# On-chip tiles that begin at multiples of 64 bytes instead of 32, in a two-layer encoder trunk

## The chip, the cores and the metric

The kernel runs on one core of one Trainium2 chip. The metric is the time of one execution on the device in microseconds (us), as the median of several runs. A profile is one execution taken by the hardware profiler; its span is the time from the first to the last instruction.

## The reference, cut to what matters

The computation is a float32 trunk of two layers over x of shape (1, 512, 1024). Each layer has a mixer with a residual add and then a feed-forward with a residual add:

```
for layer in range(2):
    h = rmsnorm(x, mix_norm[layer])
    if layer == 0:   # z = h @ e_w_in; gated short convolution (512 wide) beside
                     # sliding-window attention (8 q heads, 2 kv heads, ALiBi, sinks)
        y = concat(rmsnorm(ya, g[:512]), rmsnorm(yb, g[512:])) @ e_w_out
    else:            # z = h @ o_w_in; spatial gating over 128 positions beside
                     # latent attention (cq 384 wide, ckv 256 wide, 8 heads, rotary key)
        y = concat(rmsnorm(yc, g[:512]), rmsnorm(yd, g[512:])) @ o_w_out
    x = x + y
    h = rmsnorm(x, ffn_norm[layer])
    gate, up = split(h @ w_ffn_in[layer], 2)        # 1024 -> 2 x 2816
    x = x + (silu(gate) * up) @ w_ffn_out[layer]    # 2816 -> 1024
return x
```

## The kernel before, in words

Activations lie transposed: features on the 128 partitions, the 512 positions along the partition, so a tile of one feature block is [128, 512] float32, 2048 bytes per partition. xT holds the residual stream in 8 such blocks.

Every large product is made from three matmuls. Each operand is split in a high part, rounded to the type float32r, and a low part, the rest, in float32r too. `product` issues high x high, high x low and low x high into the same PSUM bank (lines 1506, 1507 and 1508). One operand is stationary in TensorE, the other one, 512 columns as a rule, is streamed through it (the moving operand). For plain float32 products (means of squares at line 1537, attention scores at 1881 and 1595, attention values at 1907 and 1617, the gating mix at 1870) one matmul is made in two passes. Transposes (1544, 1582, 1605, 1782, 1896, 1958) hold the data stationary and stream the identity, which is part of the tile small.

Weights come in 188 loads. SyncE's queue brings one into one of the two slots of raw, ScalarE copies it to w_hi (line 650), VectorE writes w_lo = raw - w_hi (line 1038), and TensorE uses the load (function `load`). There are four slots of w_hi and w_lo. Semaphores order this: a slot is refilled when TensorE has used it, and a raw slot when VectorE has read it. Each of the five engines runs one list of instructions in the order written, and the order around the loads is written out by hand (`through` converts up to four loads ahead).

The stages in order: x is loaded into x_tok and transposed; the first layer's projections stream h_hi and h_lo over the weights; attention and convolution of layer 0; output group over yb and ya (`out_group`); first half of the feed-forward (h streamed, 22 blocks of hidden features in act_hi and act_lo); second half (act streamed), in two passes over the output features. Layer 1 repeats this with cq and ckv as latent tiles, yc and yd ahead of the output group. In one place (columns of the spatial gate's v, loads O_CV) h is stationary and the weights stream.

The tiles' places are given by hand. `sb` places tiles one behind another from `base`: xT, h_hi, h_lo, raw, w_hi, w_lo, small, tables, gains, mix0_gain, gate_bias, sinks, eps_col, spare, mask_q, mask_k, tiny, row_scale, acc, sq, y0, rs. Behind them begins the region R (`R = place[0]`, line 160), in which the stages' tiles are laid over one another at R plus multiples of 1024 bytes: act_hi, act_lo, x_tok, e_sc, yb_hi, yb_lo, alibi, e_q, conv_y, ya_hi, cq, ckv, yc, yd, o_q, o_k, o_pT, v_c and so on. ffn_t lies over sq and y0. out_tok lies over h_hi. In the profile y0 is printed as y and mix0_gain as mix_gain.

The sizes that matter, in bytes per partition: xT 16384, h_hi and h_lo 16384 each, raw 8192, w_hi and w_lo 16384 each, small 3072, tables 6144, gains 268, mix0_gain 32, gate_bias 2048, sinks 32, eps_col 4, spare 4, mask_q and mask_k 256 each, tiny 512, row_scale and acc 2048 each, sq, y0 and rs 4096 each. The first byte that the allocator leaves free is 16481, and the end is 229344; with act_hi and act_lo (2 x 45056 bytes) behind R, the tiles reach 225824 before the change.

Of the kernel before, what the change touches and what calls it, by code (L numbers as in the profile page):

```python
# [106 lines left out]
def program(nc, x, mix_norm, ffn_norm, w_ffn_in, w_ffn_out, e_w_in, e_conv, e_q_gain, e_k_gain,  # L107
# [1 line left out]
            o_q_a_gain, o_kv_a_gain, o_w_uq, o_w_ukv, o_q_gain, o_k_gain, o_out_gain, o_w_out,  # L109
            c_small, c_tables, c_alibi, out):  # L110
    ctx = ExitStack()
    base = (nc.sbuf_base + 31) // 32 * 32
    top = nc.sbuf_top
    place = [base]

    def at(name, shape, dt, offset):
        return nc.alloc_sbuf_tensor_at(name, shape, dt, offset=offset)

    def sb(name, shape, dt=F32, size=4):
        n = size  # L120
        for d in shape[1:]:
            n *= d
        t = at(name, shape, dt, place[0])
        place[0] += (n + 31) // 32 * 32
        return t


    xT = sb("xT", [P, DT, S])
    h_at = place[0]
    h_hi = sb("h_hi", [P, DT, S], F32R)  # L130
    h_lo = sb("h_lo", [P, DT, S], F32R)
    out_tok = at("out_tok", [P, QT, D], F32, h_at)

# [1890 lines left out]
```

## Time and profile before

| what | value |
|---|---|
| median of 3 runs | 1178.49 us (1176.54 to 1180.4) |
| span of the profiled execution | 1177.5 us |
| mean granted TensorE clock | 0.995 |
| TensorE busy (matmul) | 1146.0 us, 97% |
| TensorE weight loads, beside it | 904.4 us |
| VectorE, ScalarE, GpSimd busy | 579.2, 440.9, 117.8 us |
| HBM read | 101.23 MB, 88 GB/s over the span |

How to read the rows: PE is TensorE (matmul), PEld its weight loads, DVE VectorE, ACT ScalarE, POOL GpSimd. A group of instructions names the line of the kernel, the operation, what it writes and behind the arrow what it reads; for a matmul the moving operand stands first and the stationary one second. "389" in such a row is the mean duration of one in ns. Matmuls overlap, so that the distance between two starts is shorter than the duration of one. In the chain of work that ended last each piece has its start and what it adds to the chain.

### The profile page before, as it was taken

What the parts mean: (1) busy time and instruction counts of PE and PEld (TensorE: products, weight loads), DVE (VectorE), ACT (ScalarE), POOL (GpSimd) and SP (SyncE); (2) the same over time, 40 slices, a digit from 0 to 9 for tenths busy, and PEclk for the clock granted to TensorE, in tenths of its full rate; (3) what the DMA queues carried; (4) which work ended last, traced back from release to release, by engine and by line L of the source; (5) the groups of instructions that cost most, each with busy time, mean ns of one, the idle gap of its engine ahead of it and who ended that gap; (6) DMA issues with size and microseconds to landing.
All of it is one profiled execution on the core that took longest, in us unless ns stands there. A gap on an engine that the chain in (4) does not pass through costs nothing.

```text
span 1177.5 us, 13729 instructions
## 1 busy us (share of the span) xinstructions
PE 1146.0 (97%) x5059; PEld 904.4 (77%) x5059; DVE 579.2 (49%) x796; ACT 440.9 (37%) x681; POOL 117.8 (10%) x154
## 2 busy tenths in 40 slices
PE   7999899999999999999999989999999999999998
PEld 6777668888888888888877744578888888888886
DVE  6578876534434333242675786565343443432321
ACT  5545444423223222131546666543332332321220
POOL 5010200001001000000204120000110100100000
PEclk9999999999999999999999999999999999999999
DMA  6522132232332323332323210023323323223230
GB/s 184 188 60 68 55 87 90 90 107 89 98 98 89 107 89 93 102 91 72 91 73 92 73 50 3 1 84 96 107 90 95 101 89 107 89 95 101 81 117 36
DMA packets 84983, 103.87 MB, mean 88 GB/s; under 512 B 10579, under 2 KB 61456, under 8 KB 84816
## 3 DMA queue, kind: packets, MB, share of 16 engines
q1 hardware_dynamic: 81792, 101.99, 28.5%
q10 hardware_dynamic: 2096, 1.05, 0.3%
q8 instruction: 25, 0.41, 0.2%
q0 software_dynamic: 1056, 0.30, 0.1%
q14 instruction: 14, 0.11, 0.0%
HBM read 101.23 MB, written 2.10 MB: 88 GB/s over the span
## 4 chain that ended last, share of the span: by engine, by line
PE 89%; DVE 7%; ACT 2%; DMA 1%; issue 1%; POOL 0%; SPq 0%; DVEq 0%; ACTq 0%; POOLq 0%
PE ps L1506 27%; PE ps L1507 27%; PE ps L1508 27%; PE ps L1881 2%; PE ps L1537 2%; PE ps L1907 2%; DMA x_tok<-in_x 1%; DVE e_sc L1187 1%; PE ps L1896 1%; ACT e_sc L738 1%; DVE e_sc L1176 1%; DVE tiny L1168 1%; PE ps L1883 0%; DVE e_pT L1195 0%; DVE conv_y L1236 0%
## 5 line engine op out<-in xcount | busy, mean ns | idle before, releaser
L1038 DVE TENSOR_TENSOR w_lo<-raw,w_hi 128x1024 fp32r<-128x1024 f32 (+2 forms) x194 | 228.0, 1180 | 453.9 <-ACT w_hi L650 450.9
L650 ACT ACTIVATE w_hi<-raw 128x1024 fp32r<-128x1024 f32 (+2 forms) x194 | 196.1, 1017 | 493.3 <-PE ps L1508 476.6
L1506 PE MATMUL ps<-h_hi,w_hi 128*128 128x512 f32 x928 | 367.1, 396 | 0.7 <-DVE conv_h L1207 0.6
L1508 PE MATMUL ps<-h_hi,w_lo 128*128 128x512 f32 x928 | 361.4, 389 | 0.0
L1507 PE MATMUL ps<-h_lo,w_hi 128*128 128x512 f32 x928 | 361.3, 389 | 0.0
L1506 PEld LDWEIGHTS ps<-h_hi,w_hi 128*128 128x128 f32 x928 | 174.4, 188 | 42.0 <-issue 4.6
L1507 PEld LDWEIGHTS ps<-h_lo,w_hi 128*128 128x128 f32 x928 | 174.3, 188 | 38.2 <-issue 2.6
L1508 PEld LDWEIGHTS ps<-h_hi,w_lo 128*128 128x128 f32 x928 | 174.2, 188 | 36.3
L1506 PE MATMUL ps<-act_hi,w_hi 128*128 (+1 forms) x352 | 139.6, 397 | 0.0
L1508 PE MATMUL ps<-act_hi,w_lo 128*128 (+1 forms) x352 | 139.6, 396 | 0.0
L1507 PE MATMUL ps<-act_lo,w_hi 128*128 (+1 forms) x352 | 139.5, 396 | 0.0
L543 POOL TENSOR_TENSOR ffn_t<-ffn_t,row_scale 128x512 f32<-128x512 f32 x40 | 50.8, 1291 | 558.2 <-ACT ffn_t L815 558.2
L1508 PEld LDWEIGHTS ps<-act_hi,w_lo 128*128 128x128 f32 x352 | 66.3, 188 | 16.2
L1507 PEld LDWEIGHTS ps<-act_lo,w_hi 128*128 128x128 f32 x352 | 66.3, 188 | 16.1
L1506 PEld LDWEIGHTS ps<-act_hi,w_hi 128*128 128x128 f32 x352 | 66.3, 188 | 16.1
L1290 DVE TENSOR_TENSOR ffn_t<-ps,ffn_t 128x512 f32<-128x512 f32 x44 | 30.4, 692 | 44.7 <-POOL ffn_t L543 40.6
L818 ACT ACTIVATE act_hi<-ffn_t 128x512 f32 (+1 forms) x44 | 27.8, 633 | 49.2 <-DVE ffn_t L1290 49.2
L815 ACT ACTIVATE ffn_t<-ffn_t 128x512 f32<-128x512 f32 x44 | 27.0, 633 | 39.0 <-DVE ffn_t L1286 39.0
L1293 DVE TENSOR_TENSOR act_lo<-ffn_t,act_hi 128x512 f32 (+1 forms) x44 | 30.2, 687 | 6.5 <-ACT act_hi L818 6.3
L1881 PE MATMUL ps<-o_k,o_q 128*128 128x512 f32 (+3 forms) x64 | 27.2, 509 | 4.5 <-ACT o_p L970 3.1
L1262 DVE TENSOR_TENSOR xT<-ps,xT 128x512 f32<-128x512 f32 x32 | 20.8, 682 | 20.2 <-PE ps L1508 20.2
L1286 DVE TENSOR_TENSOR ffn_t<-ps,row_scale 128x512 f32<-128x512 f32 x44 | 28.2, 681 | 0.0
(247 smaller groups left out, 1083.2 us busy)
## 6 DMA issues: line engine op xcount, KB each, us to landing
raw<-in_w_ffn_in SPq DMA_DIRECT2D x88, 512.0 KB, 3.5
raw<-in_w_ffn_out SPq DMA_DIRECT2D x44, 512.0 KB, 3.8
raw<-in_e_w_in SPq DMA_DIRECT2D x18, 512.0 KB, 3.7
raw<-in_o_w_in SPq DMA_DIRECT2D x8, 512.0 KB, 3.7
raw<-in_o_w_out SPq DMA_DIRECT2D x8, 512.0 KB, 3.6
raw<-in_e_w_out SPq DMA_DIRECT2D x8, 256.0 KB, 3.9
raw<-in_e_w_out SPq DMA_DIRECT2D x4, 512.0 KB, 4.0
out_dram<-out_tok SPq DMA_DIRECT2D x8, 256.0 KB, 3.6
```

The costliest lines, as they stand in the source:

```text
L543: pool.tensor_tensor(ffn_t[:, t, :], ffn_t[:, t, :], row_scale[:, :], ALU.mult).then_inc(silu_scaled, 1)
L650: ins = act.activation(dst, src, ACT.Copy)
L815: act.activation(ffn_t[:, b, :], ffn_t[:, b, :], ACT.Silu).then_inc(silu_done, 1)
L818: act.activation(dst[:, t, :], ffn_t[:, (t0 + t) % 4, :], ACT.Copy).then_inc(hidden_hi, 1)
L1038: ins = TT(dst, src, high, ALU.subtract)
L1286: TT(ffn_t[:, (t0 + t) % 4, :], ps[:, b0 + t, :], row_scale[:, :], ALU.mult).then_inc(gate_scaled, 1)
L1290: TT(ffn_t[:, b, :], ps[:, b0 + 2 + t, :], ffn_t[:, b, :], ALU.mult).then_inc(hidden_ready, 1)
L1293: TT(dst_lo[:, t, :], ffn_t[:, (t0 + t) % 4, :], dst_hi[:, t, :].bitcast(F32), ALU.subtract).then_inc(hidden_lo, 1)
L1506: MM(dst, st_hi, mv_hi, start=start, stop=False)
L1507: MM(dst, st_hi, mv_lo, start=False, stop=False)
L1508: return MM(dst, st_lo, mv_hi, start=False, stop=stop)
L1881: MM(s_, o_q[:, h, i * P:(i + 1) * P], o_k[:, h, 0:P * (i + 1)], start=True, stop=False)
```

## The change

Two roundings are changed: that of the first tile's start, and that of each tile's size when the next one is placed by `sb`. Tiles placed in region R are given as R plus a number and move with R. Nothing else is changed.

```diff
-    base = (nc.sbuf_base + 31) // 32 * 32
+    base = (nc.sbuf_base + 63) // 64 * 64
     top = nc.sbuf_top
     place = [base]
...
         t = at(name, shape, dt, place[0])
-        place[0] += (n + 31) // 32 * 32
+        place[0] += (n + 63) // 64 * 64
         return t
```

## Rows read from the trace of the kernel before

**Rows 1.** The page, part 1: busy time and share of each engine.
```profile
PE 1146.0 (97%) x5059; PEld 904.4 (77%) x5059; DVE 579.2 (49%) x796; ACT 440.9 (37%) x681; POOL 117.8 (10%) x154
```

**Rows 2.** The page, part 4: the chain that ended last, by engine.
```profile
PE 89%; DVE 7%; ACT 2%; DMA 1%; issue 1%; POOL 0%; SPq 0%; DVEq 0%; ACTq 0%; POOLq 0%
```

**Rows 3.** Groups, shapes apart, TensorE: line, names, shape, count | busy, mean ns | idle.
```profile
L1507 PE MATMUL ps<-h_lo,w_hi 128*128 128x512 f32 x928 | 361.3, 389 | 0.0
...
L1507 PE MATMUL ps<-act_lo,w_hi 128*128 128x512 f32 x96 | 38.0, 396 | 0.0
...
L1507 PE MATMUL ps<-yc_lo,w_hi 128*128 128x512 f32 x32 | 12.7, 396 | 0.0
...
L1507 PE MATMUL ps<-w_lo,h_hi 128*128 128x512 f32 x32 | 12.5, 390 | 0.0
...
L1507 PE MATMUL ps<-cq_lo,w_hi 128*128 128x512 f32 x24 | 9.5, 396 | 0.0
...
L1507 PE MATMUL ps<-w_lo,ckv_hi 128*128 128x256 f32 x16 | 4.5, 281 | 0.0
...
L1507 PE MATMUL ps<-ckv_lo,w_hi 128*128 128x512 f32 x8 | 3.2, 395 | 0.0
```

**Rows 4.** Timeline, TensorE, 300 to 340 us: first and last of 178 (start, us).
```profile
299.79 0.39 PE L1506 MATMUL ps<-h_hi,w_hi 128*128 128x512 f32 x1
...
339.91 0.39 PE L1506 MATMUL ps<-h_hi,w_hi 128*128 128x512 f32 x1
```

**Rows 5.** Timeline, TensorE, 500 to 540 us: first and last of 173.
```profile
499.65 0.39 PE L1506 MATMUL ps<-act_hi,w_hi 128*128 128x512 f32 x1
...
539.95 0.39 PE L1507 MATMUL ps<-act_lo,w_hi 128*128 x1
```

**Rows 6.** Chain in order of time (start, us, what): float32 means, and transposes.
```profile
634.44 1.72 PE ps L1537 x4
...
610.58 0.87 PE ps L1782 x8
```

**Rows 7.** Groups, shapes apart, ScalarE (y is y0).
```profile
L650 ACT ACTIVATE w_hi<-raw 128x1024 fp32r<-128x1024 f32 x170 | 179.5, 1057 | 471.9 <-PE ps L1508 455.2 <-DMA raw<-in_e_w_in 9.9 <-DMA raw<-in_o_w_in 4.1
...
L676 ACT ACTIVATE sq<-xT 128x512 f32<-128x512 f32 x32 | 19.7, 618 | 1.2 <-DVE acc L1069 1.1
...
L692 ACT ACTIVATE rs<-y 128x512 f32<-128x512 f32 x28 | 17.7, 632 | 3.2 <-POOL o_q L590 0.9
...
L650 ACT ACTIVATE w_hi<-raw 128x512 fp32r<-128x512 f32 x12 | 6.7, 621 | 0.0
...
L751 ACT ACTIVATE sq<-yb 128x512 f32<-128x512 f32 x4 | 2.5, 632 | 0.1
```

**Rows 8.** Groups, shapes apart, VectorE.
```profile
L1038 DVE TENSOR_TENSOR w_lo<-raw,w_hi 128x512 fp32r<-128x512 f32 x12 | 7.6, 685 | 0.0
...
L1047 DVE TENSOR_TENSOR yb_lo<-yb,yb_hi 128x512 fp32r<-128x512 f32 x4 | 2.7, 692 | 0.1
...
L1249 DVE TENSOR_TENSOR conv_y<-ps,conv_y 128x512 f32<-128x512 f32 x4 | 2.5, 680 | 0.0
```

**Rows 9.** Timeline, TensorE: idle time and its releaser, around the output groups.
```profile
157.50 1.10 PE L1537 MATMUL ps<-acc,small 128*128 128x512 f32 x2 [2.03 <-DVE acc L1080]
...
164.40 0.50 PE L1506 MATMUL ps<-ya_hi,w_hi 128*128 128x512 f32 x1 [0.19 <-DVE ya_lo L1047]
...
769.69 0.50 PE L1506 MATMUL ps<-yd_hi,w_hi 128*128 128x512 f32 x1 [0.41 <-DVE yd_lo L1047]
```

**Rows 10.** Chain, 672 to 714 us: where it leaves TensorE.
```profile
674.63 2.16 PE ps L1870 x37
676.79 0.66 DVE k_pair_a L1403
```

**Rows 11.** Windows: us, busy (x) of PE, PEld, DVE, ACT, POOL, PEclk, DMA, GB/s.
```profile
688.00:702.00 14.00, 10.58 (x39) 5.24 (x40) 12.30 (x25) 12.30 (x26) 1.39 (x2) 1.00 0.12 39
702.00:712.00 10.00, 10.00 (x21) 3.70 (x20) 8.04 (x16) 5.36 (x18) 2.12 (x1) 0.50 0.17 53
```

**Rows 12.** Chain, the start of the kernel.
```profile
2.23 9.97 DMA x_tok<-in_x
```

## The prediction

> **What bounds the kernel now.** I read four views. The page's first part says who is busy: TensorE holds 97% of the span, the next engine 49% [rows 1]. The chain of work that ended last confirms that this is the bound and not only activity: 89% of it is TensorE, 7% VectorE, 2% ScalarE [rows 2]. So anything that shortens a matmul on that chain is worth its full price, and anything on another engine is worth only what lies in the 9%. Then the groups of instructions with shapes kept apart, because a layout change can only show as a different duration of the same instruction on another tile [rows 3, 7, 8]. Last the timeline, for the distance from one start to the next, since the printed durations overlap (about 0.39 us long, 0.23 us apart) and only the distance is paid [rows 4, 5].
>
> **Where the tiles lie.** The allocator's first free byte is 16481; rounded up to 32 or to 64 it is 16512, so the first tile does not move. xT, h_hi, h_lo, raw, w_hi, w_lo, small and tables have sizes in multiples of 64, so none of them moves: they begin at 0 past a 64-byte line before and after. gains (268 bytes) is the first whose rounding changes. From gains at 115840 the sizes before are 288 + 32 + 2048 + 32 + 32 + 32 + 256 + 256 + 512 = 3488, so row_scale begins at 119328, which is 32 past a line. Everything after it has sizes in multiples of 1024, and every tile placed by hand from R is a multiple of 1024 behind R = 135712: acc, sq, y0, rs, ffn_t and the whole region R are 32 past a line. After the change the same sum is 320 + 64 + 2048 + 64 + 64 + 64 + 256 + 256 + 512 = 3648, a shift of 160 bytes: row_scale is at 119488 and R at 135872, both 0 past a 64-byte line (and, for a rival below, 64 past a 128-byte line). No instruction, wait or transfer is added or removed. The whole effect is what one start address costs an instruction.
>
> **The main term: moving operands of the three-product matmuls.** In the groups the first name behind the arrow is the operand that streams (moving), the second the stationary one. With a stream from h or w (both at 0) the mean is 389 and 390 ns; with a stream from act, yc, cq or ckv (all at 32) it is 396, 396, 396 and 395 [rows 3]. All have 512 columns and the same pair of types. The streams at 32 stand in four different stages (both output groups, the latent projections, the feed-forward's second half), those at 0 in the two others, so the stage is not what they share. The distances say the same: in the first half of the feed-forward 177 steps from 299.79 to 339.91 us, 226.7 ns each [rows 4]; in the second half 172 steps from 499.65 to 539.95 us, 234.3 ns each [rows 5]. That is 7.6 ns by distances and 7 by means; I take 7.3.
>
> Is 7.3 ns what a shift by half a 64-byte line should cost? A stream of 256 columns takes 281 ns and one of 512 takes 390, so a column costs 109/256 = 0.43 ns, and 7.3 ns are 17 columns, or 68 bytes [rows 3]. A run of 2048 bytes that begins half-way in a 64-byte line touches 33 lines instead of 32: one line more, 16 columns. ScalarE gives a second witness that knows nothing of TensorE: Square of 512 elements takes 618 ns from xT (at 0), but 632 from y0 and 632 from yb (both at 32); its cost per element is (1057 - 621)/512 = 0.85 ns, so 14 ns are again 16 elements [rows 7]. It also separates address from place, as y0 lies in the fixed part and yb in region R, and both cost the same.
>
> Count of such products: act 1056 (44 loads of 24), yb, ya, yc and yd 96 each, cq 72, ckv 24, together 1536. Not all are on the chain. In the first output group 48 products with yb end in waits: TensorE waits 2.03 us for acc and then 0.19 us for ya_lo [rows 9]. In the last load of yc before yd_lo (24 products) it waits 0.41 us [rows 9]. 12 of ckv run ahead of a stretch which the chain gives to VectorE [rows 10]. Those 84 gain nothing: the wait behind them grows by what they save. What is left is 1452 x 7.3 ns = 10.6 us. Nothing new comes late in the second half of the feed-forward: a load there would take 24 x 227 ns, which is what one takes in the first half, where the same converting work and more runs on VectorE and ScalarE and TensorE has no gap [rows 4].
>
> **The other terms.** The plain float32 products (means, scores, values) stream at another rate. Four passes of 512 columns from tiles at 32 take 1.72 us, 430 ns each; eight passes of 128 columns that stream the identity, at 0, take 0.87 us, 109 ns each [rows 6]. Between them a column costs (430 - 109)/384 = 0.836 ns, and what is left over is 2 ns for either, so a start at 32 costs these nothing I can see; bound 0 to 2 ns on the 340 or so passes of all their groups, 0 to 0.7 us, taken as 0. A stationary operand at 32 (ckv, 48 products) has no twin at 0 with 256 columns; at most the same 7 ns, 0.3 us, taken as 0. ScalarE: 2% of the chain is 24 us, of which at most 14/632 goes, 0.5 us; those of its steps that read PSUM gain nothing, so 0.4 [rows 2, 7]. VectorE: one read from PSUM and one from a tile at 32 takes 680 ns, two reads from tiles at 32 692, two at 0 685 [rows 8]; 0 to 7 ns of about 690 on 82 us of chain is 0 to 0.8 us, taken as 0. GpSimd's products are hidden, since the instructions behind them wait under TensorE's stream. The load of x into region R stands alone at the start, 9.97 us [rows 12]; no row compares starts for a DMA, so I bound it by TensorE's own 1.8% either way, 0.2 us, taken as 0. The clock: between 702 and 712 us the granted clock is 0.50, behind a stretch in which TensorE was busy for 10.58 of 14 us [rows 11]; the change shortens this stretch by 0.1 us at most, so I leave the drop where it is.
>
> Sum: 10.6 + 0.4 = 11.0 us. Against the profiled execution, 1177.5 us of span, that is 1166.5. The median of the runs is 1178.49, which is 1.0 above this span, so the forecast is 1167.5 us.
>
> **A rule that speaks against it.** The rows show a cost for a start at 32. The Trainium skill ("SBUF — State Buffer", in the notes under Door 1) states lines of 16 bytes for SBUF, with a price for each access that crosses to a new line; by it 32 and 64 are both whole lines, the sum would be 0, and the time 1178.5. The rows differ, as 396 against 389 ns shows. The same page ("Operand start alignment") only says what starts are legal and that its runs timed nothing.
>
> **The rivals.**
> 1. The start is not the cause. If the 7 ns came from something else that region R's tiles share (their place high in the partition, or the neighbour that writes them), or only a multiple of 128 bytes is a good start, nothing is gained: all tiles that now stream fast begin at 0 past a 128-byte line too, and after the change region R begins at 64 past one. Time 1178.5. For it: no row has a stream that begins at 64 past 128, so the trace can't exclude it. Against it: y0 and yb agree although only one is in R [rows 7], and an extra line of 128 bytes would be 32 columns, 13.8 ns, twice what is measured. This is also what would be seen if the change did not move the tiles as I computed.
> 2. Slower: the cost grows with the bytes ahead of the start within a 128-byte line. Then 32 bytes cost 7.3 ns and 64 cost 14.6; all 1452 products on the chain pay 7.3 more, 10.6 us, and the time is 1189.1. It decides if the memory fetches 128 bytes at a time and throws the head away. Against it: 32 bytes are 8 columns, which at 0.43 ns are 3.4 ns, half of the measured.
> 3. The clock. The drop of 10 us at half speed costs 5 us of work [rows 11]. If the slightly shorter wait keeps the clock up, the time is 1162.5; if the shift makes another such stretch, in the attention of the first layer, 1172.5.
>
> **How the numbers follow.** The forecast, 1167.5, has a chance of 0.82; rival 1 0.09; rival 2 0.03; rival 3 0.03 on either side. The range takes in the bounds (7.0 to 7.6 ns, the 0.8 us of VectorE, 0.7 of plain float32 and 0.2 of the load) and both ends of the clock: 1162 to 1173, which leaves out rivals 1 and 2. About 0.3%, 3.5 us, is what a measurement of this kernel can tell from no change. Faster by more: 0.82 + 0.06 = 0.88; within it: 0.09; slower: 0.03.
>
> **What would show it.** In the profile of the changed kernel the streams from act, yb, ya, yc, yd, cq and ckv should read 389 to 390 ns, those from h and w stay at 389 and 390, and the second half of the feed-forward should step at 227 ns, so that each of its four halves is 264 x 7.3 ns = 1.9 us shorter. Square from y0 and yb should read 618, the pass of 512 float32 columns still 430. If act still reads 396, rival 1 holds, at 403 rival 2. The prediction is wrong as a sum if act reads 389 and the span is still above 1170: then a wait ahead of an output group or the clock took the gain back.

## The result, and the profile after

The changed kernel takes 1172.03 us (median of 4 runs, 1170.75 to 1172.07) against 1179.05 us (4 runs, 1176.54 to 1180.4) for the kernel before: a ratio of 0.9934 with a 95% interval of 0.9919 to 0.9949. It is faster by 7.0 us by the medians, 7.8 by the ratio. The forecast was 1167.5 in a range of 1162 to 1173. The direction and the place of the gain were right. The price per product was not (5.4 ns from start to start instead of 7.3), and the experiments show that the reason given for it was wrong altogether.

The page of the profile after, parts 1 and 4, as [rows 1] and [rows 2]:

```profile
span 1170.2 us, 13729 instructions
...
PE 1139.3 (97%) x5059; PEld 905.5 (77%) x5059; DVE 578.3 (49%) x796; ACT 440.6 (38%) x681; POOL 118.2 (10%) x154
...
PE 92%; DVE 5%; DMA 1%; ACT 1%; issue 1%; POOL 0%; ACTq 0%; DVEq 0%; POOLq 0%
```

TensorE lost 6.7 us of busy time, 1146.0 to 1139.3, and the other engines nothing to speak of. The groups of TensorE, shapes apart, which answer to [rows 3]:

```profile
L1507 PE MATMUL ps<-h_lo,w_hi 128*128 128x512 f32 x928 | 362.4, 391 | 0.0
...
L1506 PE MATMUL ps<-act_hi,w_hi 128*128 128x512 f32 x96 | 37.9, 394 | 0.0
L1508 PE MATMUL ps<-act_hi,w_lo 128*128 128x512 f32 x96 | 37.6, 392 | 0.0
L1507 PE MATMUL ps<-act_lo,w_hi 128*128 128x512 f32 x96 | 37.3, 389 | 0.0
```

The reader should see that the three products of one triple now differ: 394, 389 and 392 ns, where the product with act_lo alone had come down to the 389 of h. If a start at 64 cured the stream, all three would read 389. The timeline, first and last of 177 (start, us), which answers to [rows 5]:

```profile
499.70 0.39 PE L1508 MATMUL ps<-act_hi,w_lo 128*128 128x512 f32 x1
...
539.99 0.39 PE L1507 MATMUL ps<-act_lo,w_hi 128*128 x1
```

176 steps of 228.9 ns, against 234.3 before and 226.7 for h. And ScalarE, which answers to [rows 7]:

```profile
L676 ACT ACTIVATE sq<-xT 128x512 f32<-128x512 f32 x32 | 19.7, 618 | 1.1 <-DVE acc L1069 1.1
...
L692 ACT ACTIVATE rs<-y 128x512 f32<-128x512 f32 x28 | 17.7, 633 | 3.2 <-POOL o_q L590 0.9
...
L751 ACT ACTIVATE sq<-yb 128x512 f32<-128x512 f32 x4 | 2.5, 631 | 0.1
```

y0 and yb now begin at 0 past a 64-byte line, and Square from them still takes 633 and 631 ns. The second witness of the prediction has withdrawn its statement.

### The profile page after: what moved, and what is told of

Its sections match the earlier page's. It is cut to its first block, busy times and chain, and to the rows that moved or that the text cites. A ratio compares the mean times of both kernels' runs of the same rounds, so it can differ in the third digit from the quotient of the medians.

```text
span 1170.2 us, 13729 instructions
## 1 busy us (share of the span) xinstructions
PE 1139.3 (97%) x5059; PEld 905.5 (77%) x5059; DVE 578.3 (49%) x796; ACT 440.6 (38%) x681; POOL 118.2 (10%) x154
## 3 DMA queue, kind: packets, MB, share of 16 engines
q0 software_dynamic: 1056, 0.30, 0.1%
## 4 chain that ended last, share of the span: by engine, by line
PE 92%; DVE 5%; DMA 1%; ACT 1%; issue 1%; POOL 0%; ACTq 0%; DVEq 0%; POOLq 0%
PE ps L1506 28%; PE ps L1508 28%; PE ps L1507 28%; PE ps L1881 2%; PE ps L1537 2%; PE ps L1907 1%; DMA x_tok<-in_x 1%; PE ps L1896 1%; DVE e_sc L1187 0%; PE ps L1605 0%; PE ps L1883 0%; DVE e_pT L1195 0%; PE ps L1617 0%; DVE e_sc L1176 0%; PE ps L1958 0%
## 5 line engine op out<-in xcount | busy, mean ns | idle before, releaser
L1038 DVE TENSOR_TENSOR w_lo<-raw,w_hi 128x1024 fp32r<-128x1024 f32 (+2 forms) x194 | 228.9, 1185 | 448.4 <-ACT w_hi L650 445.3
L1507 PE MATMUL ps<-act_lo,w_hi 128*128 (+1 forms) x352 | 136.7, 388 | 0.0
```

The source lines that it names most:

```text
L1038: ins = TT(dst, src, high, ALU.subtract)
L1507: MM(dst, st_hi, mv_lo, start=False, stop=False)
```

## The experiments

### A kernel of cases, and three layouts

```diff
# starts_alone: one case of the kernel of cases; d is the stream's offset in bytes
+        for b, c, first, last in banks(2):
+            MM(b, w_hi[:, c:c + P], m_hi[:, d // 4:d // 4 + 512], start=first, stop=False)
+            MM(b, w_hi[:, c:c + P], m_lo[:, d // 4:d // 4 + 512], start=False, stop=False)
+            MM(b, w_lo[:, c:c + P], m_hi[:, d // 4:d // 4 + 512], start=False, stop=last)
```

> A kernel that computes nothing of the reference (its output is zeros). It repeats the three-product pattern (high x high, high x low, low x high, 512 columns, four PSUM banks) 48 times per case, with the stream beginning at +0, 16, 32, 48, 64, 96, 128, 160, 192, 256 and 512 bytes from a multiple of 1024, then the same with the stream's tiles high in the partition (+0, 32, 64, 96, 128), then with the stationary operand at +32, 64, 96 and the stream at 0 or at the same offset. ScalarE takes Square of 512 elements at +0, 32 and 64 from a tile low, in the middle and high in the partition. Theory of the 64-byte line (the one on record): 227 ns from start to start at +0, 64, 128, 192, 256, 512, and 234 at +16, 32, 48, 96, 160; stationary offset without effect; Square 14 ns longer at +32 than at +0 and +64. Theory of the 128-byte line (the changed kernel's 229 ns steps at 64 past 128 and unchanged ScalarE speak for it): 227 only at multiples of 128, 229 at +64 and +192, 234 at +32, +96, +160; Square the same at all starts of one place. Theory of the relation (what counts is where the stream lies against the stationary operand): with stationary and stream both at +32 the step is 227 again, and stationary +32 with stream +0 gives more than 227.

(The cut writes the kernel's literal offsets with d; the operands are all zeros.) Measured: steps from the starts in the trace, over the 48 products of a case without its first six (w is the stationary operand, m the stream; the granted clock is 1.00):

| stream | stationary | step, ns |
|---|---|---|
| +0 | +0 | 226.7 |
| +16 | +0 | 231.6 |
| +32 | +0 | 233.3 |
| +48 | +0 | 233.4 |
| +64 | +0 | 228.8 |
| +96 | +0 | 233.4 |
| +128 | +0 | 233.4 |
| +160 | +0 | 234.2 |
| +192 | +0 | 233.4 |
| +256 | +0 | 227.2 |
| +512 | +0 | 226.7 |
| +0 | +32, +64, +96 | 233.4, 233.3, 234.4 |
| +32, +64, +96 | the same | 226.7 each |

With the stream's tile high in the partition, +0, 32, 64, 96 and 128 give 226.7, 233.3, 228.8, 233.4 and 233.4, as low in it. Four of the cases in the timeline, first and last of 48 each: stream and stationary at +0; stream +128; stationary +32 with the stream at +0; both at +32.

```profile
31.62 0.39 PE L105 MATMUL ps<-m_hi,w_hi 128*128 128x512 f32 x1
42.27 0.39 PE L107 MATMUL ps<-m_hi,w_lo 128*128 128x512 f32 x1
...
98.23 0.40 PE L129 MATMUL ps<-m_hi,w_hi 128*128 128x512 f32 x1
109.20 0.39 PE L131 MATMUL ps<-m_hi,w_lo 128*128 128x512 f32 x1
...
209.16 0.39 PE L169 MATMUL ps<-m_hi,w_hi 128*128 128x512 f32 x1
220.11 0.40 PE L171 MATMUL ps<-m_hi,w_lo 128*128 128x512 f32 x1
...
220.34 0.40 PE L173 MATMUL ps<-m_hi,w_hi 128*128 128x512 f32 x1
231.00 0.40 PE L175 MATMUL ps<-m_hi,w_lo 128*128 128x512 f32 x1
```

The four stretches are 10.65, 10.97, 10.95 and 10.66 us long. The stream of the third pair begins at a multiple of 1024 bytes and is slow; that of the fourth begins at 32 past one and is fast. So no alignment of the stream makes the speed. What counts is where the streams lie against the stationary operands. Both at +0, +32, +64 or +96 give 226.7; a stationary operand at +32, +64 or +96 under a stream at +0 (224, 192 and 160 modulo 256) gives 233.4, 233.3 and 234.4, where streams displaced by as much over a stationary one at +0 give 233.4 (in starts_fine), 233.4 and 234.2; and +256 and +512 are as fast as +0 within 0.5 ns. Of the layouts of this kernel, stream minus stationary modulo 256 (the relation, from here on) is 0 for h, 160 for region R before (135712 - 73856 = 61856) and 64 for it after (62016), for which the cases give 226.7, 234.2 and 228.8, against 226.7, 234.3 and 228.9 in the kernels.

ScalarE in the same kernel, from tiles low, in the middle and high in the partition (groups; line 64 is +0 low, 70 +64 low, 73 and 76 are +0 and +32 in the middle, 85 is +32 high), and one of them in the view by tile:

```profile
L76 ACT ACTIVATE squares<-mid 128x512 f32<-128x512 f32 x8 | 4.3, 618 | 0.0
...
L85 ACT ACTIVATE squares<-high 128x512 f32<-128x512 f32 x8 | 4.3, 617 | 0.0
...
L73 ACT ACTIVATE squares<-mid 128x512 f32<-128x512 f32 x8 | 4.3, 617 | 0.0
L64 ACT ACTIVATE squares<-low 128x512 f32<-128x512 f32 x8 | 4.3, 614 | 0.0
```

```profile
L70 ACT ACTIVATE squares<-low x8: 614/616/632, 16.3 to 20.0; 128x512 f32<-128x512 f32 x8
```

Neither start nor place matters. In every group of eight the first instruction, which waits for the group before, reads 629 to 633 ns, and the seven behind it 612 to 617 (the last row has min, median and max). An instruction that finds ScalarE idle behind a wait reads some 16 ns more, whatever it reads from; and in the kernel Square from y0 and yb does so each time (idle 32 ns or more before each of the 28 and the 4). The trace of the kernel before could have shown it, since Square from xT, at 0 past a line, has both values. ScalarE's timeline there, one that is queued and two behind idle time:

```profile
15.71 0.61 ACT L676 ACTIVATE sq<-xT 128x512 f32<-128x512 f32 x1
...
22.15 0.63 ACT L676 ACTIVATE sq<-xT 128x512 f32<-128x512 f32 x1 [0.53 <-DVE acc L1069]
...
24.01 0.63 ACT L676 ACTIVATE sq<-xT 128x512 f32<-128x512 f32 x1 [0.53 <-DVE acc L1069]
```

```diff
# shift_all_32: every tile 32 bytes on
-    base = (nc.sbuf_base + 31) // 32 * 32
+    base = (nc.sbuf_base + 31) // 32 * 32 + 32
```

> The kernel before with its first tile 32 bytes further on, so that every tile moves by 32 and no tile moves against another: h, w, raw and xT are now at 32 past a 64-byte line, region R and the tiles before it at 0 past 64 (64 past 128). Theories of a line (64 or 128): the streams from h and w (2880 products) now step at 234 instead of 227 ns, those from region R (1536) at 229; about +22 - 8 = +14 us, a span of 1191 to 1193. Theory of the relation between stream and stationary operand: nothing changes, 227 and 234 ns where they were, span 1177.5.

Measured: span 1175.4 us, 1177.21 us of time beside a median of 1178.89 for the kernel before. In its timeline 177 steps of h from 299.65 to 339.77 us are 226.7 ns each, 171 steps of act from 499.78 to 539.84 us 234.3 ns. Every start has changed and no step. Both theories of a line expected some 14 us more.

```diff
# round_128: both roundings at 128
-    base = (nc.sbuf_base + 31) // 32 * 32
+    base = (nc.sbuf_base + 127) // 128 * 128
...
-        place[0] += (n + 31) // 32 * 32
+        place[0] += (n + 127) // 128 * 128
```

> Both roundings at 128 bytes instead of 64: the tiles from xT to gains stay, region R begins at a multiple of 128. Theory of the 64-byte line, with 2 ns of the step from another cause: as the changed kernel, 1172.0, streams from act step at 229 ns. Theory of the 128-byte line: they step at 226.7 ns like those from h, another 1452 x 2.3 ns = 3.3 us, so 1168.7 and a ratio to before of 0.991.

Measured: 1176.95 us (12 runs), ratio 0.9984 (0.9974 to 0.9995). The timeline, first and last of 173:

```profile
499.78 0.40 PE L1508 MATMUL ps<-act_hi,w_lo 128*128 128x512 f32 x1
...
539.91 0.40 PE L1506 MATMUL ps<-act_hi,w_hi 128*128 x1
```

233.3 ns. R lies at 136192, 128 modulo 256 from the weights, where the cases have 233.4. A stricter alignment than the change's, which it contains, keeps a quarter of the gain.

```diff
# region_only_64: region R alone, 32 bytes on
-    R = place[0]
+    R = place[0] + 32
```

> The kernel before with 32 bytes put between rs and region R, and nothing else: R is at 0 past 64 as in the changed kernel, while row_scale, acc, sq, y0, rs and ffn_t stay at 32. If the whole gain is the streams from region R, this gives the gain of the changed kernel, a ratio to before of 0.994; if the fixed tiles carry a part of it, less.

Measured: 1177.18 us (12 runs), ratio 0.9986 (0.9974 to 0.9998), act again at 233.3 ns (499.84 to 539.97 us, 172 steps). Here every tile of region R begins at a multiple of 64, as in the changed kernel, and the gain isn't there. The relation is 192, for which the cases have 233.4. Neither of the two outcomes that were expected came, since both took the multiple of 64 as the cause.

### The relation put to the test

```diff
# region_0
-    R = place[0]
+    R = place[0] + 96
```

> The kernel before with 96 bytes put between rs and region R, so that R's tiles begin at the same place modulo 256 as w_hi and w_lo. Theory of the relation (the step depends on stream minus stationary, modulo 256; 0 gives 226.7 ns in the kernel of cases, 64 gives 228.8, 160 gives 234.2): act, ya, yb, yc, yd, cq, ckv step at 226.7, 1452 x 7.5 ns = 10.9 us less than before, 1168 us, a ratio of 0.991, better than the changed kernel. Theory that the good start of the changed kernel is its 64-byte multiple: R is now 0 past 128, which gained nothing in round_128, so again a ratio of 0.998.

Measured: 1167.53 us (5 runs, 1166.89 to 1169.23), ratio 0.9909 (0.9894 to 0.9923), half a microsecond from what was expected, and faster than the changed kernel, by some 3 us going by the two ratios. The changed kernel's place of region R, measured in the same stretch of runs (region_64 below), has no run under 1170.21, this one none above 1169.23. The timeline, first and last of 178, and the group beside it:

```profile
499.76 0.39 PE L1508 MATMUL ps<-act_hi,w_lo 128*128 128x512 f32 x1
...
539.88 0.39 PE L1508 MATMUL ps<-act_hi,w_lo 128*128 x1
```

```profile
L1506 PE MATMUL ps<-act_hi,w_hi 128*128 x256 | 99.7, 390 | 0.0
L1507 PE MATMUL ps<-act_lo,w_hi 128*128 x256 | 99.7, 389 | 0.0
L1508 PE MATMUL ps<-act_hi,w_lo 128*128 x256 | 99.6, 389 | 0.0
```

226.7 ns per step and all three products alike.

```diff
# region_64
-    R = place[0]
+    R = place[0] + 160
```

> The kernel before with 160 bytes put between rs and region R and nothing else: R where the changed kernel has it, all tiles from gains to rs where the kernel before has them. Theory of the relation: steps of 232, 226 and 229 ns for the streams from R, 1452 x 5.3 ns = 7.7 us, a ratio of 0.9935 as for the changed kernel, since no other engine gains from the fixed tiles. If the fixed tiles carry a part, less.

Measured: 1171.77 us (6 runs), ratio 0.9941 (0.9927 to 0.9956), act at 228.9 ns (176 steps from 499.67 to 539.95 us). The intervals of this ratio and of the changed kernel's overlap: the move of region R alone gives the gain, and the tiles from gains to rs, which here lie where the kernel before has them, carry no part that shows. Between this run and region_0 lie 4.2 us, where 1452 products at 2.2 ns are 3.2.

```diff
# weights_moved
+    place[0] += 160
     w_hi = sb("w_hi", [P, W_SLOTS, 1024], F32R)
```

> The kernel before with 160 bytes put between raw and w_hi. w_hi, w_lo and everything behind them move by 160, so region R keeps its distance to the weights (160 modulo 256), and h_hi and h_lo, which do not move, are now 96 modulo 256 from them. All starts of the weights stay multiples of 32, those of h multiples of 128. Theory of the relation: the 2784 products that stream h step at 233.4 ns instead of 226.7, the 96 that stream the weights over h at 234, those of region R stay at 234; 18.7 + 0.7 us, a span of some 1195 to 1197. Theory of absolute starts: h has not moved and R has the relation it had but other starts, so h stays at 227; span 1170 to 1178.

Measured: span 1193.3 us, time 1195.13 (one run), some 17 us slower than the kernel before (median 1178.17). The timeline, first and last of 173, of the stage of [rows 4]:

```profile
299.67 0.39 PE L1507 MATMUL ps<-h_hi,w_hi 128*128 128x512 f32 x1
...
339.80 0.40 PE L1508 MATMUL ps<-h_lo,w_hi 128*128 128x512 f32 x1
```

h has not moved by a byte, and its steps went from 226.7 to 233.3 ns. The expected 1195 to 1197 was 2 to 4 us too high for the span; the count of 2784 took every h product as on the chain, and the trace shows where that fails: the 432 of the first layer's projections at 6.6 ns would be 2.9 us, but the first products of the feed-forward that follows come only 0.4 us later (h_lo's at 198.9 instead of 198.5 us).

The last run is a second kernel of cases, in finer steps, with parts of the triple displaced alone, with shorter streams and with plain float32:

```diff
# starts_fine: three kinds of its cases
+            MM(b, w_lo[:, c + 32:c + 32 + P], m_hi[:, 0:512], start=False, stop=last)     # only w_lo +128
...
+            MM(b[:, 0:256], w_hi[:, c:c + P], m_hi[:, 16:16 + 256], start=first, stop=False)  # 256 columns, +64
...
+            MM(b, p_w[:, c:c + P], p_m[:, 8:8 + 512], start=first, stop=False)            # plain float32, +32
```

> A kernel that computes nothing of the reference (its output is zeros): the three-product pattern, 48 per case, with the streams 0 to 256 bytes from the stationary operands in steps of 16, and 8 and 4; then only w_lo or only m_lo displaced by 128, 64 and 32; then streams of 256 and 128 columns; then plain float32 operands. Theory of the relation: 226.7 ns at 0 and 256 alone, 228.8 at 64, 231 to 234 elsewhere. If what counts is the weight load that runs beside a stream (the one for the next product), displacing w_lo alone slows only the step of the product ahead of it, and displacing m_lo alone one step in three; if it is the product's own stationary operand, the step of the product with w_lo. Shorter streams: the same cost per step if it comes from the weight load's 128 columns, half or a quarter of it if it comes from the stream's length. Plain float32: 0 to 2 ns per pass at any relation.

Measured, steps in ns as before:

| case | step |
|---|---|
| +0, 16, 32, 48 | 226.7, 231.6, 233.3, 233.4 |
| +64, 80, 96, 112 | 228.8, 231.1, 233.4, 231.3 |
| +128, 144, 160, 176 | 232.5, 233.3, 234.2, 233.3 |
| +192, 208, 224, 240, 256 | 233.4, 234.6, 233.4, 226.7, 226.9 |
| +4, +8 | 236.6, 233.3 |
| only w_lo +128 / only m_lo +128 | 231.0 / 229.0 |
| only w_lo +64 / only m_lo +64 | 231.0 / 232.2 |
| only w_lo +32 / only m_lo +32 | 233.5 / 233.4 |
| 256 columns, +0, 64, 128, 160 | 120.0, 117.8, 118.7, 117.3 |
| 128 columns, +0, 64, 128, 160 | 111.6, 111.7, 111.6, 111.7 |
| plain float32 passes, +0, 32, 64, 128, 160 | 429.2 each |

Two runs of one case can differ: +128 is 232.5 here and 233.4 in starts_alone, +256 226.9 and 227.2. Two things were not expected: +240 is as good as 0, and with 256 columns the relation 0 is the slowest of the four (by 1 to 3 ns), not the fastest. So the cost is neither a constant of a weight load nor in proportion to the stream: the relation that is fastest with 512 columns is slowest with 256 and makes no difference with 128. Why is not shown. With only w_lo displaced by 128 the steps behind high x high are 226.7, behind high x low 232.6 and behind low x high 234.0; with only m_lo displaced the step behind high x low alone rises, to 234.4, and the others stay at 226.6 and 225.7. In the first case both the product beside which w_lo is loaded and the product that uses it are slow, so this does not tell the two apart. And with only m_lo displaced by 64 all three steps rise, to 231.9, 232.4 and 232.2, more than when both streams are displaced by 64 (228.8 in the mean). So a product's step isn't given by its own two operands alone: the relation is shown for a triple whose streams are displaced together, as in every layout of this kernel. Why addresses matter at all, and whether it is reads of the memory that collide, is left open. Plain float32 pays nothing at any relation, as the prediction had it.

## Why the prediction was right, and where it was wrong

The number lies in the range, and the mechanism is not the predicted one. That there was a gain at all is luck: rounding to 64 bytes happened to bring region R from relation 160 to 64, and with R 128 bytes lower or 320 higher (region_only_64, round_128; multiples of 64 both times) the same theory would have forecast as much and found 1.7 to 1.9 us. So is part of the hit: 1172.03 lies in the range only because of the 5 us left for the clock (by the other bounds it would have ended near 1169), while of the 4.5 us between forecast and result the price explains 2.8 (1452 x 1.9 ns) and ScalarE 0.4.

**What moves, and by how much.** Right: region R by 160 bytes, nothing ahead of gains. This arithmetic is also what later explained every run, once it was applied to differences.

**The witness of h against act.** The rows were right and the reading wrong. All fast streams began at 0 past 64 and all slow ones at 32, but they also all had relation 0 and relation 160 to the weights. The stages that were compared could not tell the two apart, since w stands at the same residue in all of them. The row that seemed to, with h stationary and w streaming at 390, has relation 0 too.

**The agreement of 17 columns and 16 elements.** A coincidence, twice. Relation 160 costs 7.5 ns; but relations 128 and 192, whose streams begin at a whole line of 64 bytes and touch no line more, cost 5.8 to 6.7, and relation 64 costs 2.1. ScalarE's 14 ns is there at any start: 618 against 632 was not a pair that differs in its start alone, as Square from y0 and yb also stands behind a wait each time.

**The main term.** The step that failed is the price after the change: 226.7 ns were taken, 228.9 came. 1452 x (234.3 - 228.9) = 7.8 us instead of 10.6. ScalarE's 0.4 us came to 0. The prediction's own sign, act at 389, came for one product of three (394, 389, 392), and neither of the other two signs, 396 or 403, for any. The count of products on the chain held: region_0, where the price is the full 7.5 ns, came out 10.6 us below the kernel before, beside 1452 x 7.5 = 10.9; that its 1167.53 is also the forecast of this change is chance. VectorE (692 ns before, 693 after for the same steps) and plain float32 were rightly taken as 0. For plain float32 the working did not show it: a line through two points leaves the same rest, 2 ns, at both, whatever a start costs; starts_fine shows it (429.2 ns at five relations).

**The clock.** The drop behind [rows 11] did not stay as it was: it began at 700.8 us and lasted 6.8 us instead of 10.2, and three short ones came in the first layer. Windows of the profile after (us, busy and count of PE, PEld, DVE, ACT, POOL, granted clock, DMA, GB/s):

```profile
700.80:707.60 6.80, 6.80 (x13) 2.55 (x14) 6.45 (x13) 2.49 (x5) 1.82 (x1) 0.50 0.24 77
158.10:161.50 3.40, 3.33 (x6) 2.04 (x7) 2.36 (x2) 2.10 (x3) 0.00 (x0) 0.50 0.11 37
89.80:93.20 3.40, 3.40 (x13) 3.01 (x13) 3.33 (x5) 1.66 (x5) 0.00 (x0) 0.50 0.12 41
14.70:18.10 3.40, 3.40 (x13) 3.00 (x12) 3.30 (x6) 3.35 (x7) 3.12 (x6) 0.50 0.55 155
```

They are not the change's: shift_all_32, with the steps of the kernel before, has one of them too, and a drop of 6.8 us at 702.4. What sets their number and length is not shown. In this one profile they put the first layer back and the shorter one gives some of it back later. The view by tile shows the balance, with first and last start of ya_hi's and act_hi's products, the first pair of rows from the kernel before and the second from after:

```profile
L1506 PE MATMUL ps<-ya_hi,w_hi x32: 392/397/496, 164.4 to 197.5; 128*128 128x512 f32 x32
...
L1508 PE MATMUL ps<-act_hi,w_lo x352: 392/397/403, 439.0 to 1169.0; 128*128 x128, 128*128 128x512 f32 x48
```

```profile
L1506 PE MATMUL ps<-ya_hi,w_hi x32: 393/394/395, 166.2 to 198.5; 128*128 128x512 f32 x32
...
L1508 PE MATMUL ps<-act_hi,w_lo x352: 391/392/396, 440.0 to 1161.7; 128*128 x128, 128*128 128x512 f32 x48
```

Behind by 1.8 us at the first ya product and by 1.0 at the first of act, ahead by 7.3 at the last: 8.3 us are gained from there on, of which act's 1056 products at 5.4 ns are 5.7, the 252 other products of the second layer on the chain 1.4, and the rest, 1.2, is no more than the shorter drop can give (3.4 us less at half speed, 1.7 us of work).

**The rivals.** The rival that named "something else that region R's tiles share" was the right one in its cause, though neither of its examples (the place, the neighbour that writes) was it, and wrong in its outcome: it concluded that a wrong cause means no gain. What R's tiles share is their distance to the weights, and the change altered that distance, to a value that happens to be better. The rival of the 128-byte line was wrong in both forms. The one that ended slower had the wrong mechanism, but its kind of outcome exists: 160 bytes ahead of w_hi instead of behind it cost 17 us.

**The rule of 16-byte lines.** The Trainium skill ("SBUF — State Buffer", under Door 1) states lines of 16 bytes, and was cited as speaking for no gain. The steps do change between starts that are all multiples of 16 (226.7, 231.6, 233.3, 233.4 at +0, 16, 32, 48 from the stationary operand), so that by itself it does not give them; nothing here shows whether such lines are what collides.

## What to carry to other kernels

When two groups of instructions differ in duration and their tiles differ in the start, write down the address of every operand and compare the differences of addresses before calling it alignment; the cheapest test is to move everything together. In a stream of 512-column float32r products, each with its own weight load, put the moving tiles at the same residue modulo 256 bytes as the stationary ones: here that is 96 bytes of padding for 0.9% (1167.5 against 1178.2 us), and a careless 160 bytes in another place cost 1.4%. For other widths measure first: with 256 columns that relation was the slowest of four. A supporting observation on another engine is one only if its pair of rows differs in nothing but the thing claimed; an agreement of magnitudes alone has misled here twice.

## What the runs showed of the hardware

In triples of 512-column float32r products, each with its weight load and the streams displaced together, TensorE's mean step depends on the moving operand's start minus the stationary operand's start modulo 256 bytes: 226.7 to 227.2 ns at 0 (and 226.7 at 240), 228.8 at 64, 231 to 235 at the other multiples of 16, 233.3 at 8 and 236.6 at 4. With one operand of the triple displaced alone it is 229 to 233.5. The absolute starts and the place in the partition do not matter in any case tried. Steps fall into short repeating patterns, for instance 232, 226 and 229 ns at relation 64. Streams of 256 columns differ by up to 2.7 ns, and relation 0 is the slowest there (120.0 against 117.3 at 160); those of 128 columns (111.6 or 111.7) and plain float32 (429.2) do not differ. Square of 512 elements on ScalarE takes 612 to 617 ns from any start tried, and 629 to 633 as the first instruction behind a wait.
